# Two-network transformer kernel: pieces of a convolution moved between the halves of a level, a projection's weights split beside a norm, and three merged edits (tap placement, last norm and output, stick-breaking attention)

## What is computed

```python
def wkv7_scan(r, w, k, v, a, b):                 # per token; the kernel solves it in chunks of 128
    sa = einsum('bhvk,bhk->bhv', state, a_t)
    state = state * w_t + sa * b_t + v_t * k_t ; y_t = einsum(state, r_t)
def conformer_conv_module(h, ...):
    u = glu(h @ w_pw1 + b_pw1)
    u = causal_dwconv(u, dw_w, dw_b)             # 31 taps, 1024 channels, 256 tokens
    return silu(layer_norm(u)) @ w_pw2 + b_pw2
def stick_breaking_layer(h, w_qkv, w_out):       # 16 heads of 64
    z = q @ k.T * 64 ** -0.5                     # valid: key before query
    neg = where(valid, softplus(z), 0)
    later = reversed_cumsum(neg) - neg
    a = where(valid, exp(log_sigmoid(z) - later), 0)
    return (a @ v) @ w_out
x = layer_norm(alpha * x + (1 + gate2) * ffn, g, b)    # the last line of the last layer is the output
```

## Time and profile before

| what | value |
|---|---|
| median of 3 runs | 2697.58 us (2695.21 to 2702.38) |
| the profiled execution's own time | 2701.74 us |
| its span | 2700.0 us |
| granted TensorE clock, mean | 0.952 |
| PE, DVE, ACT, POOL busy | 91%, 72%, 54%, 0% |
| HBM read | 458.85 MB, 170 GB/s over the span |

### The profile page before, as it was taken

How to read it: one execution, slowest core, us unless ns; L and a number is a source line. 1 busy time by engine, 2 the same in 40 slices (tenths; PEclk the granted TensorE clock), 3 DMA queues, 4 the chain that set the end, 5 groups by cost and what they waited for, 6 DMA issues and landing times. The chain is left out here.

```text
span 2700.0 us, 46670 instructions
## 1 busy us (share of the span) xinstructions
PE 2462.3 (91%) x18974; PEld 2333.8 (86%) x18974; DVE 1951.2 (72%) x3277; ACT 1449.4 (54%) x2632; POOL 12.8 (0%) x20
## 2 busy tenths in 40 slices
PE   7898999988989999799998979999988999977998
PEld 6688999977889999789998879997788999855997
DVE  5476788754867886668887768886459888757885
ACT  6444555355445553656744556746464674524663
POOL 0000000000000000000000000000000000000000
PEclk8799999988999999899999989999989999988999
DMA  5122668731135577214565624573334457611452
GB/s 212 47 94 104 225 222 303 302 110 60 66 142 216 210 307 297 96 46 141 195 258 219 233 84 155 199 297 108 141 111 172 149 195 296 264 63 63 173 199 82
DMA packets 63654, 462.91 MB, mean 171 GB/s; under 512 B 7184, under 2 KB 7376, under 8 KB 7504
## 3 DMA queue, kind: packets, MB, share of 16 engines
q1 hardware_dynamic: 63440, 459.92, 45.8%
HBM read 458.85 MB, written 1.05 MB: 170 GB/s over the span
## 5 line engine op out<-in xcount | busy, mean ns | idle before, releaser
L751 PE MATMUL psum<-arena_rounded,upper_rounded 128*128 128x256 f32 (+2 forms) x5112 | 1454.4, 285 | 123.4 <-PEq L652 40.4
L752 PE MATMUL psum<-arena_rounded,upper_rounded 128*128 128x256 f32 (+2 forms) x5112 | 1441.5, 282 | 0.0
L753 PE MATMUL psum<-arena_rounded,ring_rounded 128*128 128x256 f32 (+2 forms) x5112 | 1440.5, 282 | 0.0
L751 PEld LDWEIGHTS psum<-arena_rounded,upper_rounded 128*128 128x128 f32 (+2 forms) x5112 | 978.2, 191 | 143.0 <-issue 81.6
L567 DVE TENSOR_TENSOR ring_rounded<-ring,upper_rounded 128x1024 fp32r<-128x1024 f32 (+4 forms) x958 | 840.8, 899 | 356.8 <-ACT upper_rounded L558 352.3
L558 ACT ACTIVATE upper_rounded<-ring 128x1024 fp32r<-128x1024 f32 (+4 forms) x958 | 750.8, 795 | 587.1 <-PE psum L753 485.9
L752 PEld LDWEIGHTS psum<-arena_rounded,upper_rounded 128*128 128x128 f32 (+2 forms) x5112 | 981.9, 192 | 0.7 <-issue 0.5
L753 PEld LDWEIGHTS psum<-arena_rounded,ring_rounded 128*128 128x128 f32 (+2 forms) x5112 | 979.2, 192 | 0.0
L589 DVE SCALAR_TENSOR_TENSOR ada_sum<-ring,small,ada_sum 128x1024 f32<-128x1024 f32 x168 | 215.1, 1281 | 2.4 <-DMA ring<-stream_dram 1.1
L2482 DVE SCALAR_TENSOR_TENSOR arena<-psum,cols,arena 128x255 f32<-128x255 f32 (+1 forms) x352 | 153.3, 478 | 57.3 <-ACT arena L2449 54.2
L2449 ACT ACTIVATE arena<-psum,cols 128x256 f32<-128x256 f32 x176 | 89.4, 560 | 73.0 <-PE psum L753 73.0
(11 more groups left out here) (521 smaller groups left out, 2538.8 us busy)
## 6 DMA issues: line engine op xcount, KB each, us to landing
ring<-stream_dram SPq DMA_DIRECT2D x434, 1024.0 KB, 4.8
const<-const_dram SPq DMA_DIRECT2D x1, 1540.0 KB, 14.9
x<-x_dram SPq DMA_DIRECT2D x1, 1024.0 KB, 4.8
out_dram<-x SPq DMA_DIRECT2D x1, 1024.0 KB, 3.9
cols<-cols_dram SPq DMA_DIRECT2D x1, 978.0 KB, 11.7
const<-const_dram SPq DMA_DIRECT2D x1, 67.0 KB, 4.5
pos<-positions_dram SPq DMA_DIRECT2D x1, 64.0 KB, 6.0
cols<-cols_dram SPq DMA_DIRECT2D x1, 4.0 KB, 4.3
```

Of the source, the lines that this page charges most:

```text
L751: pe.matmul(out, upper, x[0][:, b.k, :], start=(b.k == 0), stop=False)
L752: pe.matmul(out, upper, x[1][:, b.k, :], start=False, stop=False)
L753: ins = pe.matmul(out, lower, x[0][:, b.k, :], start=False, stop=(b.k == nk - 1))
```

## The change

Five edits. **(1)** In the levels of the recurrence, the transposes and the two convolution blocks now stand between the two groups of half products instead of behind both. **(2)** After the square of the group norm ACT emits the splits that chunk `conv_end[4]` allows, and DVE does its part at the end of its list there; before, they came with the first step of `conv_o`. **(3)** The conformer's tiles on PE are 3, 5, 7 instead of 2, 3, 4, 7; DVE has (0, 1), (2, 4), (6,); PE's taps stand ahead of tiles 10, 12, 14, and the diagonals are made later. **(4)** In the last norm ACT applies gain and shift, and four transfers send x in quarters from the same block. **(5)** Stick-breaking: v's projection, the attention and the out-projection are one block; v's matmuls stand between the attention's; the mask is added to the scores; the split of the result is done by pairs of tiles; `sb_out` does its first four tiles together; at the end of `sb_qk` both engines emit the splits of one more chunk. Three functions without a caller go away (`split_tiles`, `project_tokens`, `norm`).

```diff
-            g["sb_out", i] = by_rounds(matrix("sb_w_out_2", (0,), D, tiles(0, KD)))
+            g["sb_out", i] = by_rounds(matrix("sb_w_out_2", (0,), D, tiles(0, KD)), TOGETHER)
...
-        "strict": np.concatenate([p < f, np.ones((P, P)), p < f], 1),
+        "strict": p < f,
+        "strict_add": np.concatenate([np.where(p < f, 0.0, NEG), np.zeros((P, P))], 1),
...
                     ins.then_inc(half_ready, 1)
-                if n == 1:
...
-                if n == 2:
...
-                if n >= 3:
-                    pe.wait_ge(turned_copied, 2)
-                    conv(pe, 2)
+                    if b == 0 and n == 1:
...
+                    if b == 0 and n == 2:
...
+                    if b == 0 and n >= 3:
+                        pe.wait_ge(turned_copied, 2)
+                        conv(pe, 2)
...
+            w.dve(dve, conv_end[4])
...
             act.activation(y, y_centred, ACT.Square, scale=1.0 / 8).then_inc(squared, 1)
+            w.act(act, conv_end[4])
...
-            for k in range(KD if not last else 0):
+            for k in range(KD):
                 act.wait_ge(normed, k + 1)
+                if last:
+                    act.activation(xs[:, k, :], xs[:, k, :], ACT.Identity, scale=gain[:, k:k + 1],
+                                   bias=shift[:, k:k + 1]).then_inc(lower_ready, 1)
+                    continue
...
+    if last:
+        @st.block.sync
+        def _(sp):
+            for n in range(KD // 2):
+                part = slice(2 * n * T, 2 * (n + 1) * T)
+                sp.wait_ge(lower_ready, 2 * (n + 1))
+                sp.dma_start(chip.out[:, part], chip.x[:, part]).then_inc(chip.out_written, 16)
...
-    on_pe, on_dve = (2, 3, 4, 7), ((0, 1), (5, 6))
+    on_pe, on_dve = (3, 5, 7), ((0, 1), (2, 4), (6,))
+    diagonals_by = (4, 8, 14, 20, 38, 56, 75, len(pe_taps))
...
-                    for tile, n in pe_taps[made:(m + 1) * len(pe_taps) // KD]:
+                    for tile, n in pe_taps[made:diagonals_by[m]]:
...
-            taps(pe, 2 * TAPS_CC, 2 * TAPS_CC)
+            taps(pe, TAPS_CC + half, 2 * TAPS_CC - half)
...
-                inserts={8: lambda pe: taps(pe, 0, half), 10: lambda pe: taps(pe, half, TAPS_CC - half),
-                         12: lambda pe: taps(pe, TAPS_CC, half),
-                         14: lambda pe: taps(pe, TAPS_CC + half, TAPS_CC - half)})
+                inserts={10: lambda pe: taps(pe, 0, half), 12: lambda pe: taps(pe, half, TAPS_CC - half),
+                         14: lambda pe: taps(pe, TAPS_CC, half)})
...
+            w.act(act, s["last"])
...
+            w.dve(dve, s["last"])
...
+            scores(0)
+            scores(1)
+            values(0, range(KD))
+            sums(0)
+            sums(1)
+            values(1, range(KD // 2))
+            pe.wait_ge(v_taken, NT)
+            weighted(0)
+            scores(2)
+            weighted(1)
+            scores(3)
+            values(1, range(KD // 2, KD))
+            sums(2)
+            sums(3)
+            pe.wait_ge(v_taken, 2 * NT)
+            weighted(2)
+            weighted(3)
...
+            def mask(g):
...
+                for part, add in masks:
+                    dve.scalar_tensor_tensor(part(z), part(ps), scale, add, ALU.mult, ALU.add).then_inc(masked, 1)
...
+            w.dve(dve, last_of(1))
+            take(2)
+            take(3)
+            lower_of(2)
+            lower_of(3)
+
+        def entry(pe, step):
+            pe.wait_ge(out_taken, len(groups))
...
-        with stage(chip) as (block,):
-            @block.sync
-            def _(sp):
-                sp.dma_start(out, chip.x[:, :]).then_inc(chip.out_written, 16)
-                sp.wait_ge(chip.out_written, 16)
```

More of the change, by code:

```diff
@@ L783, in project @@
     return s
[L786 to L801, removed]
 def store_with_act(dst):
@@ L816, in store_with_act @@
     return epilogue
[L819 to L825, removed]
-        @block.sync
-        def _(sp):
[L829 to L859, removed]
-                act.wait_ge(w.used, end + 1)
-                act.activation(dst(0, n), chip.bank(n * NT, blocks[n * nk].width), ACT.Identity)
-        @block.vector
[L864 to L868, removed]
-                dve.wait_ge(w.used, end + 1)
-                dve.tensor_copy(dst(1, n), chip.bank(n * NT + 1, blocks[n * nk].width))
@@ L2402, in whole_of @@
                 dve.wait_ge(normed, k + 1)
[L2403 to L2408 removed]
+                chain(dve.tensor_scalar(lower[:, k, :], xs[:, k, :], h_gain[:, k:k + 1], h_bias[:, k:k + 1],
+                                        ALU.mult, ALU.add))
             def lower_of(k):
@@ L3599, in out, with scores @@
-    def out(st):
-        x = chip.split(slot2(chip, 5), o)
-        return ("sb_out", i), KD, x, split_tiles(st, o, x, KD), None
+            def scores(g):
+                ps, (c0, _) = scores_of(g), groups[g]
+                if g >= 2:
+                    pe.wait_ge(out_taken, g - 1)
+                for c in range(per_group):
+                    pe.matmul(first(ps)[:, c, :], qk[rows_of(g), KD + c0 + c, 0:P], qk[rows_of(g), c0 + c, :],
+                              start=True, stop=True)
+                    ins = pe.matmul(second(ps)[:, c, :], qk[rows_of(g), KD + c0 + c, P:T], qk[rows_of(g), c0 + c, P:T],
+                                    start=True, stop=True)
+                ins.then_inc(scores_ready, 1)
@@ new lines, in values @@
+            def values(n, ks):
+                if n and ks[0] == 0:
+                    pe.wait_ge(v_taken, NT)
+                for k in ks:
+                    at = n * KD + k
+                    b = blocks[at]
+                    if at == 0 or blocks[at - 1].chunk is not b.chunk:
+                        pe.wait_ge(w.lower_ready, b.chunk.order + 1)
+                    upper, lower = w.parts(b)
+                    for tt in range(NT):
+                        sl = slice(tt * P, (tt + 1) * P)
+                        pe.matmul(v_bank(tt), h[0][:, k, sl], upper, start=(k == 0), stop=False)
+                        pe.matmul(v_bank(tt), h[0][:, k, sl], lower, start=False, stop=False)
+                        ins = pe.matmul(v_bank(tt), h[1][:, k, sl], upper, start=False, stop=(k == KD - 1))
+                    if b is b.chunk.end:
+                        ins.then_inc(w.used, 1)
```

338 lines of the change are left out of this document (154 added, 184 removed).

## The result

The changed kernel took **2671.36 us** (median of 4 runs, 2670.53 to 2672.31), the kernel before 2699.98 beside it (2695.21 to 2705.18): ratio **0.9894**, 95% interval 0.9873 to 0.9914. The forecast was 2654.7 (2645 to 2669), so the direction is right and the time lies 2.4 us outside the range. Two later comparisons on other chips gave medians of 2658.66 and 2666.45, ratios 0.9861 (0.9836 to 0.9886) and 0.9866 (0.9837 to 0.9895); both medians lie inside the range, so on which side of 2669 the time falls is chance. All 14 runs of the changed kernel have the median 2666.7 (2657.2 to 2672.3), 52 of the kernel before about 2701 (2685.4 to 2712.0): **34 us** less where 42.9 were forecast. The profiled execution took 2670.53, its span 2668.5.

A forecast was written before the change was run, and what follows sets the result against it. PE, busy 91% of the span, was taken as the bound, with gains from removed matmuls, waits and low-clock time. Terms 6.7 + 0.9 + 8.2 + 23.7 + 3.4 = 42.9 us off 2697.58 gave 2654.7 us, range 2645 to 2669.

The forecast's parts named there:

- the two spacings of 0.3: Group norm, layer 0: ACT time taken out ahead of DVE's norm work, priced at 0.5 us of edit 2's 0.9.
- every mark of it: Conformer signs: centring 8 us sooner, DVE without a gap from step 3, PE waiting about 9 us before tile 7.
- hand-overs: Attention: some 25 passes between engines; each 0.2 us longer than taken would cut edit 5's gain to 18 us.
- scores 3: Attention: group 3's scores wait for take 1, queued on DVE behind mask 2; PE waits 2 to 3 us.
- sums 2: Attention: sums for group 2, cold at 5.6 us, after a PE wait of 4 to 5 us.
- the late entry: Attention's start: scores begin 2.2 us late, after 3.8 us of standing, because the added split's block end holds all engines.
- The failing terms: Attention's low-clock prices: 4.8 us for the first group of scores and 5.6 us for the sums of group 2.
- If the clock falls elsewhere: Sign of a wrong prediction: the clock falling in places other than those forecast; no size given.
- The bank wait: Out-projection: doing four tiles together makes tile 4 wait for a bank, priced at +0.8 us.
- attention half: Rival: the attention's many hand-overs and DVE's fixed order leave 12 us gained instead of 23.7, total 2666; chance 0.12.
- the rival with the clock gate: Rival: the attention's matmuls stay at 1.2 GHz through the whole block, 53 us more, total 2708; chance 0.02.
- a gain in one stretch is not given back in the next: Sum of all edits: five stretches don't overlap and the weight ring is full at each start, so 42.9 us stands.

The follow-up runs named there:

- kept_busy_short: Changed kernel plus useless matmuls (6, 2, 4, 8 and 11) in TensorE's attention waits; median 2649.15 us, ratio 0.9816 to the kernel before.
- after_third: The changed kernel, unchanged, profiled a third time beside its variants; profiled execution 2669.41 us.
- after_again: The changed kernel, unchanged, profiled a second time; profiled execution 2658.16 us, ratio 0.9861 to the kernel before.
- after: The changed kernel with all five edits, first trace; profiled execution 2670.53 us, ratio 0.9894 to the kernel before.

## Why the prediction missed

**Edit 1 held.** 6.2 us of the 6.7; levels of 6.17 us where 6.15 was forecast. The convolution and the transposes lie where they cost nothing.

**Edit 2 was undersized**: 1.5 us for 0.9. The step itself held: in layer 0 DVE begins its norm work 3.77 us after `conv_o`'s first matmul (235.92 - 232.15) instead of 4.38 (237.16 - 232.78), 0.6 sooner for the two spacings of 0.3. PE's waits did not shrink, 0.87 and 1.67 us behind DVE where 2.24 stood. What the sum had at nothing is the clock: no fall in this stretch (1.00 for 0.83), which is what is left for the other 0.3 us per layer; that share is argued, not measured by a run of its own.

**Edit 3 held**: 8.0 us for 8.2 (9.4 in the changed kernel, with more of the last taps at full clock), and every mark of it: the chain of 29 taps took 15.07 us, 0.52 each as taken from the earlier trace rows, PE waits 8.53 for the 9 forecast, and both ends meet. By the Trainium skill (VectorE: DVE Perf Modes, section The DRAIN you can't avoid) chained and paired operations would be equally far apart; 0.52 here against 0.40 of the earlier trace rows says otherwise: an operation that waits for the one just before it costs 0.12 us more than one of a pair.

**Edit 4 was a little undersized**: 4.0 us for 3.4. The last quarter landed in 2.0 us, not the 2.6 that I had set in the middle of its bounds.

**Edit 5 is the step that failed**: 17.4 us for 23.7. The order of the block, its hand-overs and its waits came as forecast (2.2 ahead of scores 3 and 4.1 ahead of sums 2 in the second trace, for 2 to 3 and 4 to 5), and so did the late entry, 3.0 us for 3.6. The failing terms are those of the clock. The working held 4.3 us for it: 4.8 instead of 2.5 for the first scores, 5.6 instead of 3.6 for the sums of group 2. Take them out and it has 16.1, 40.4, 52.7 and 72.5 for the last four lines of the table above; `kept_busy_short`, at full clock throughout, has 16.2, 40.8, 53.5 and 73.1. So the hand-overs, some 25 of them, were right to 0.6 us in sum, and the clock costs the changed kernel 6.4 to 9.5 us of this chain, not 4.3.

I had let PE be warm after 4.8 us of scores, by the earlier trace rows, where the clock had come back after 4 us of work. Here it came back 11 to 14 us after the first score, behind both groups of scores and 6 to 11 of v's products. That made the sums of group 0 2.6 to 4.2 us later than forecast, and all of it in the chain, since PE went from v's last product to these sums without a wait. The kernel before had a warning in the same block: behind its wait of 12.99 us PE still ran at half for all of the next 5.9 us.
```profile
2402.30:2408.20 5.90, 5.90 (x13) 3.55 (x14) 3.43 (x3) 0.00 (x0) 0.00 (x0) 0.50 0.00 0
```
In two of three executions of the changed kernel the stretch is 3 us longer still: there the clock fell again, in the first of them at 2387, though PE had stood for only 1.31 us between short groups just before. "If the clock falls elsewhere" was among the signs of being wrong.

The rest of edit 5's miss has two parts. The stretch of the kernel before that I read, 105.05 us, was the longest of five (104.1 on average): 1.0 us. And the out-projection with its norm takes 36.5 us instead of 34.4, 2.1 more where 1.0 was priced. The bank wait is 0.67 of it (0.8 forecast). The other 1.4 us stand at its end, behind its last matmul (12.37 us to the next stage's first one, 10.98 before): one more weight split stands on DVE ahead of the last tile's copy, and PE waits for it. The half clock at its start (0.71 over the first 5 us) is no part of the difference, since the kernel before had it too (0.66). DVE and PE:
```profile
2452.95 1.22 DVE L569 TENSOR_TENSOR ring_rounded<-ring,upper_rounded 128x1024 fp32r<-128x1024 f32 x1
2454.09 0.48 DVE L2234 SCALAR_TENSOR_TENSOR x<-psum,ada,stat 128x256 f32<-128x256 f32 x1
...
2454.62 0.70 PE L2190 MATMUL psum<-x,const 128*128 128x256 f32 x2 [0.85 <-DVE x L2234]
```
The rival "attention half" (12 us) named the right place, but blamed the hand-overs; the rival with the clock gate named the right cause at more than ten times its size (53 us beyond the forecast's own term, against 2.1 to 5.2). I should have given the lesser form of it a price in the sum. The Trainium skill (TensorE: Matmul & The Clock Gate, section HAM oscillation — how this bites in real kernels) describes such falls behind waits; the runs agree in kind, and show that a kernel with short groups between short waits pays it as well.

**The sum.** 6.2 + 1.5 + 8.0 + 17.4 + 4.0 = 37.1 us where 42.9 stood, and 37.3 is what the traces give once the pace is taken out; that they agree so closely is luck, given the 5.5 us between two traces of one kernel. So 6 of the missing 14 us (42.9 against 28.6 in the first comparison) are the attention's. Over all runs 9 are missing (34 for 42.9), since the first comparison had the slowest of the changed kernel's three medians. The rest was in a sentence that I took for safe, that a gain in one stretch is not given back in the next. No edit was seen to give it back, but the profiled execution had 2215 more matmuls at the slow pace than the one of before, 9.8 us. For the other three runs of that comparison no trace exists, so for their median the pace is only argued. The forecast was also hung on 2697.58, the median of three runs, where 52 have about 2701. Single runs of one kernel on one chip spread by up to 25 us, and the medians of the changed kernel by 13 between chips, so a range of 24 us around a sum of terms would be missed now and then even if each term had been right.

## What to carry to other kernels

Price the clock where a block of short matmul groups comes behind a wait of 3 us: the first 11 to 14 us ran at half speed here, and useless matmuls in the waits, sized by their own duration and ending before the wait does, brought back 6.4 to 9.5 us of 83 to 86. A split or a copy added ahead of a block's end held every engine (PE stood 3.02 us with it, 1.33 without); put it behind, where its engine would wait anyway. Before an untouched stretch is blamed or trusted, profile the same kernel twice.

## What the runs showed of the hardware

At a granted clock of 1.00 the split 128x256 matmuls have two paces, 113.3 and 117.8 ns from start to start, mostly constant for ten microseconds or more at a time (up to 186), and one program takes different ones from execution to execution. Over 14 traces of ten kernels 6224 to 9969 of some 14,700 matmuls were at the slower pace, 17 us between the ends. The granted clock doesn't show it. A page of the Trainium skill (TensorE: Matmul & The Clock Gate, section Back-to-back issue gap) has for an isolated matmul of 256 columns one warm spacing, 262 cycles, or 109 ns; neither pace is that. The clock itself also fell at different places in different executions of one kernel: the second fall, at 2387, is in `after_third` too (0.66 over 2383 to 2403), but absent in `after_again`. It does so outside the change as well: from 2053 to 2061 the granted clock is 1.00 in `after` and 0.79 in `after_third`, and the same matmuls take 1.5 us longer there. Outside the stretches that the edits touch, and without the pace, the 14 traces lie between 2153.6 and 2161.2 us.
